# The first block's input stage done chunk by chunk, its loads moved to other queues, and a rewritten sliding softmax

## The reference

```
h = rms_norm(x, norm1_g) * (1 + scale1) + shift1
proj = h @ w_in                       # q_g k_g v_g a_lr r_g q_s k_s v_s
log_a = log_sigmoid(a_lr @ w_alpha + b_alpha) / 16
o_gla = rms_norm(gla_mixer(q_g, k_g, v_g, log_a)) * silu(r_g)
o_swa = rms_norm(swa_mixer(q_s, k_s, v_s, sinks))
x = x + gate1 * (concat(o_gla, o_swa) @ w_out)
x = x + gate2 * peer_mixer(modulate(x, ...))     # 256 x 8 x 16 expert rows looked up in a table
```

## Time and profile before

| | us |
|---|---|
| median of 3 runs | 1480.1 (1479.36 to 1480.94) |
| profiled execution: its own time, which is its span | 1480.7 |
| PE busy | 1311.9 (89%) |
| DVE busy | 933.9 (63%) |
| ACT busy | 655.4 (44%) |
| stage that the change touches | 0 to about 122 us of the span |

### The profile page before, as it was taken

How to read it: one execution, slowest core, us unless ns; L and a number is a source line. 1 busy time by engine, 2 the same in 40 slices (tenths; PEclk the granted TensorE clock), 3 DMA queues, 4 the chain that set the end, 5 groups by cost and what they waited for, 6 DMA issues and landing times.

```text
span 1480.7 us, 21207 instructions
## 1 busy us (share of the span) xinstructions
PE 1311.9 (89%) x6932; PEld 936.0 (63%) x6932; DVE 933.9 (63%) x2248; ACT 655.4 (44%) x1801; POOL 390.6 (26%) x432
## 2 busy tenths in 40 slices
PE   6999979888988777878777887999999998999998
PEld 3889934444443222333222476999998987899897
DVE  6678586766667667667754555655556635655555
ACT  3434434344343333333333335545455248544554
POOL 4111144444544444444444142200001005100000
PEclk9999999999999999999999998999999999999999
DMA  8875599999999999999999621665556630445554
GB/s 332 333 254 200 182 422 420 421 421 421 421 421 422 421 422 421 422 421 422 421 422 421 268 89 37 234 219 182 182 182 238 196 102 14 157 149 188 187 185 144
DMA packets 81341, 422.51 MB, mean 285 GB/s; under 512 B 10144, under 2 KB 11472, under 8 KB 48368
## 3 DMA queue, kind: packets, MB, share of 16 engines
q0 software_dynamic: 46656, 303.71, 50.1%
q1 hardware_dynamic: 33280, 114.68, 23.3%
q10 hardware_dynamic: 1328, 3.15, 0.6%
HBM read 418.88 MB, written 2.62 MB: 285 GB/s over the span
## 4 chain that ended last, share of the span: by engine, by line
PE 55%; DMA 27%; DVE 8%; ACT 5%; issue 2%; POOL 1%; DVEq 0%; ACTq 0%; SPq 0%; POOLq 0%
DMA big<-in_experts,R 26%; PE pacc L1136 8%; PE pu L663 6%; PE pu L664 6%; PE pu L665 6%; PE pu L632 3%; DVE big L2380 3%; PE pu L644 2%; PE pacc L663 2%; PE pacc L664 2%; PE pacc L665 2%; PE pacc L720 2%; PE pacc L722 2%; PE pacc L721 2%; ACT L1455 1%
## 5 line engine op out<-in xcount | busy, mean ns | idle before, releaser
L1136 PE MATMUL pacc<-big,early_l 128*128 128x512 f32 x1024 | 492.7, 622 | 119.5 <-ACT early_l L1455 119.2
L1136 PEld LDWEIGHTS pacc<-big,early_l 128*128 128x128 f32 x1024 | 188.1, 195 | 408.4 <-issue 406.1
L2380 DVE CUSTOM_DVE_ANT_0 big<-big,early_h 128x1024 f32<-128x1024 f32 x256 | 311.8, 1224 | 204.9 <-DMA big<-in_experts,R 203.8
L535 POOL DMA_INDIRECT big<-in_experts,R x256 | 288.1, 1125 | 378.7 <-PE pacc L1136 334.3
L436 DVE TENSOR_TENSOR ring_lo<-ring,ring_hi 128x512 fp32r<-128x512 f32 x328 | 214.7, 696 | 195.0 <-ACT ring_hi L429 194.9
L429 ACT ACTIVATE ring_hi<-ring 128x512 fp32r<-128x512 f32 x328 | 187.6, 620 | 123.5 <-PE pu L665 49.4
L1455 ACT ACTIVATE R<-R 128x1 f32<-128x1 f32 x256 | 51.6, 202 | 322.3 <-DVE R L2380 322.1
L663 PE MATMUL pu<-X2h,ring_hi 128*128 128x256 f32 x512 | 146.2, 286 | 3.2 <-DVE big L2497 3.2
L665 PE MATMUL pu<-X2h,ring_lo 128*128 128x256 f32 x512 | 145.6, 284 | 0.0
L664 PE MATMUL pu<-X2l,ring_hi 128*128 128x256 f32 x512 | 145.4, 284 | 0.0
L663 PEld LDWEIGHTS pu<-X2h,ring_hi 128*128 128x128 f32 x512 | 98.9, 193 | 4.2 <-DVE big L2497 3.6
(11 more groups left out here) (408 smaller groups left out, 2097.4 us busy)
## 6 DMA issues: line engine op xcount, KB each, us to landing
ring<-in_weights SPq DMA_DIRECT2D x216, 512.0 KB, 3.5
big<-in_ada POOLq DMA_DIRECT2D x40, 512.0 KB, 6.3
big<-in_w POOLq DMA_DIRECT2D x12, 512.0 KB, 7.1
big<-in_experts,R POOLq DMA_INDIRECT x256, 20.0
bias_row<-big ACTq DMA_DIRECT2D x1, 1536.0 KB, 19.8
XT<-in_xT ACTq DMA_DIRECT2D x1, 1024.0 KB, 8.2
scr<-in_ada POOLq DMA_DIRECT2D x2, 512.0 KB, 12.3
tk<-in_ada POOLq DMA_DIRECT2D x2, 512.0 KB, 14.0
```

The lines of the kernel that those rows point to most:

```text
L535: pool.indirect_dma_start(out=pair_rows[:, m % PAIR_SLOTS, :], out_offset=None, in_=experts_d, in_offset=bass.IndirectOffsetOnAxis(ap=expe ...
L1136: last = mm(paccf[:, tt * D + half * 512:tt * D + (half + 1) * 512], diagonal[:, m % 16, :], pair_rows[:, m % PAIR_SLOTS, D + half * 512:D ...
L2380: v.tensor_tensor_reduce(out=pair_rows[:, m % PAIR_SLOTS, 0:D], in0=pair_rows[:, m % PAIR_SLOTS, 0:D], in1=h2_rows[:, u % TT, :], scale=1. ...
```

## The change

1. Eight chunks of `w_in` (q, k, v of the sliding mixer and q of the linear one) are laid out by chunk of x: slot c has the rows of chunk c for 8 output tiles. PE adds all 8 tiles in PSUM (`pacc`) as each chunk comes, the narrow product with them. ACT copies 8 tiles out at the end. `EARLY` becomes 8, `BESIDE` 9.
2. The 16 first modulation rows come as 8 pairs of 1 MB, loaded from ACT's queue, with columns, bias table and one-hot table in front; c, x in two halves and weight slots 0 to 7 from SP's queue; the other small loads from POOL's.
3. The bias row is made by one product for 8 partitions, and the store repeats each row 128 times by a step of 0.
4. 24 matmuls on zeros stand at PE's start. The sum of squares is taken in two halves. DVE scales x chunk by chunk.
5. Sliding softmax: ACT makes a table of slope times distance per head; DVE makes the negated logits with their minimum in one instruction (`negative_logits`) and a one-column minimum with the negated sink.
6. The decay arithmetic of DVE becomes filler of steps 0 to 5, in front of it nothing; the exponentials of ACT come in three parts after slots 10 to 12. Modulation rows fill steps 6 to 16, five follow.

```diff
-EARLY, BESIDE = 6, 11
+EARLY, BESIDE = 8, 9
+EXPS_AFTER = 10
@@ SP
-            for dst, src, sem in ((cols[:, :], cols_d, "cols_loaded"), ...
-            for k in range(RING):
-                if k < 2:
-                    sp.wait_ge(s["ada_used"], 8 + 4 * k)
-                sp.dma_start(ring[:, k, :], weights_d[k, :, :]).then_inc(slot_full[k], 16)
+            sp.dma_start(cs, c_d.partition_broadcast(P)).then_inc(s["c_loaded"], 16)
+            for half, sem in enumerate(("x_loaded", "x_late_loaded")):
+                sp.dma_start(XT[:, 4 * half:4 * half + 4, :], xT_d[:, 4 * half:4 * half + 4, :]).then_inc(s[sem], 16)
+            for c in range(C):
+                if c >= RING:
+                    sp.wait_ge(s["slots_used"], c + 1 - RING)
+                ring_load(c)
@@ POOL
-            for n_row in range(2 * C):
-                pool.dma_start(mod_row(n_row), ada_d[n_row, :, :]).then_inc(ada_first[first_part(n_row)[0]], 16)
+            for dst, src in ((walr, small_d[:, :, 0:16]), (walpha[0:16, :], alpha_d), (sinks[:, :], sinks_d.partition_broadcast(P)),
+                             (keysT, keys_d)):
+                pool.dma_start(dst, src).then_inc(s["small_loaded"], 16)
@@ PE
+            full_array(24, pu[:, 1, 0:T])
+            pe.wait_ge(s["cols_loaded"], 16 * 3)
+            mm(pu[0:NH, 0, 0:BROW], relb[0:NB, 0:NH], oneh[0:NB, :], start=True, stop=True).then_inc(s["row_psum"], 1)
...
+            pe.wait_ge(s["small_loaded"], 16 * 4)
+            pe.wait_ge(s["row_copied"], 1)
             for c in range(C):
                 pe.wait_ge(s["h_chunks"], c + 1)
+                last = mm(pn[0:16, 0:T], walr[:, c, :], HTf[:, c, :], start=(c == 0), stop=(c == C - 1))
...
+                wait_slot(c)
+                w = slot(c)
+                for j in range(7):
+                    last = mm(pacc[:, j, :], w[:, j * P:(j + 1) * P], HTf[:, c, :], start=(c == 0 and j % 2 == 0),
+                              stop=(c == C - 1), skip_group_check=True)
+                    if c == C - 1 and j == 4:
+                        log_decay()
+                for tt in range(TT):
+                    last = mm(pacc[:, 7, tt * P:(tt + 1) * P], HTf[:, c, tt * P:(tt + 1) * P], w[:, 7 * P:C * P], start=False,
+                              stop=(c == C - 1), skip_group_check=True)
+                last.then_inc(s["slots_used"], 1)
@@ ACT
+            for dst, src in ((cols[:, :], cols_d), (relb[0:NB, :], relb_d), (oneh[0:NB, :], onehot_d)):
+                act.dma_start(dst, src).then_inc(s["cols_loaded"], 16)
+            for c in range(6):
+                pair_load(c)
...
+            act.wait_ge(s["row_psum"], 1)
+            f(brow[0:NH, 0, :], pu[0:NH, 0, 0:BROW], ACT.Copy).then_inc(s["row_copied"], 1)
             act.wait_ge(s["sums"], NORM["n1"])
             f(R[:, 0:TT], pn[:, 0:TT], ACT.Sqrt, scale=1.0 / D, bias=eps[:, 0:1]).then_inc(s["roots"], 1)
+            act.wait_ge(s["row_copied"], 1)
+            row = brow[0:NH, 0, 0:1]
+            act.dma_start(row_dram, bass.AP(tensor=row.tensor, offset=row.offset, ap=[list(row.ap[0]), [0, P], [1, BROW]]))\
+                .then_inc(s["row_stored"], 16)
+            for c in range(6, C):
+                act.wait_ge(ada_pair[c - 6], 16)
+                pair_load(c)
+            act.wait_ge(s["consts_made"], 1)
+            for h in range(SH):
+                f(swa_table[:, h, :], ndist, ACT.Copy, scale=2.0 ** (-8.0 * (h + 1) / SH))
             for c in range(C):
                 act.wait_ge(s["h_scaled"], c + 1)
                 f(HTf[:, c, :], HTf[:, c, :], ACT.Identity, bias=mod[:, 2 * c + 1:2 * c + 2], ...
...
+            act.wait_ge(s["slots_used"], SLOT["w_in"] + C)
+            for j in range(4):
+                f(qs[:, j, :], pacc[:, j, :], ACT.Copy, scale=float(SD) ** -0.5).then_inc(s["evacs"], 1)
+            f(ks, pacc[:, 4, :], ACT.Copy).then_inc(s["evacs"], 1)
...
@@ DVE
+            def normed_chunk(c):
+                dve.wait_ge(s["ada_used"], 2 * c + 2)
+                v.tensor_tensor(mod[:, 2 * c:2 * c + 2], mod[:, 2 * c:2 * c + 2], first[:, 2 * c:2 * c + 2], ALU.add)
+                v.scalar_tensor_tensor(HTf[:, c, :], XT[:, c, :], column("n1", c), pm[:, 0:T], ALU.mult, ALU.mult)\
+                    .then_inc(s["h_scaled"], 1)
+            modulation(0, 2)
+            dve.wait_ge(s["roots"], NORM["n1"])
+            v.reciprocal(R[:, 0:TT], R[:, 0:TT]).then_inc(s["inverses"], 1)
+            modulation(2, 2)
+            dve.wait_ge(s["spreads"], 1)
+            normed_chunk(0)
+            normed_chunk(1)
+            for c in range(2, C):
+                modulation(2 * c, 2)
+                normed_chunk(c)
...
+            def negative_logits(u, S, ps, added):
+                v.tensor_tensor_reduce(out=S, in0=ps, in1=added, scale=-1.0, scalar=3.0e38, op0=ALU.add, op1=ALU.min,
+                                       accum_out=stats[:, u % 4:u % 4 + 1]).then_inc(s["att_biased"], 1)
...
-                v.tensor_copy(Ssw[:, u % 4, L:L + 1], sinks[:, h:h + 1])
-                v.scalar_tensor_tensor(S, ndist[:, T - L:T], 2.0 ** (-8.0 * (h + 1) / SH), ps, ALU.mult, ALU.add)\
-                    .then_inc(s["att_biased"], 1)
+                negative_logits(u, S, ps, swa_table[:, h, T - L:T])
             def swa_filler(i):
-                if i < 12:
-                    modulation(2 * C + 6 + i, 1)
-                if 8 <= i < 8 + 3 + NSUB:
-                    gla_product(i - 8)
+                if i < 6:
+                    decay_part(i)
+                else:
+                    modulation(2 * C + i, 1)
+                if 11 <= i:
+                    gla_product(i - 11)
+                if i == 16:
+                    gla_product(i - 10)
...
-            modulation(2 * C + 18, 4)
+            modulation(2 * C + 17, 5)
```

More of the change, by code:

```diff
@@ L97 @@
 NORM = {n: i + 1 for i, n in enumerate(NORMS)}
[L98 removed]
+SQUARED = {n: i + 2 for i, n in enumerate(n for n in NORMS if n not in ("n2", "n2_late", "fin", "attn0", "lat", "mlp0", "attn1", "mlp1"))}
 def attention_units():
@@ L797, in attend, with full_array @@
                     one(step)
+            def full_array(count, out):
+                for _k in range(count):
+                    mm(out, zeros[:, 0:P], zeros[:, :], start=True, stop=True)
             pe.wait_ge(s["casts_made"], 1)
[L801 to L804, removed]
+            full_array(24, pu[:, 1, 0:T])
+            pe.wait_ge(s["cols_loaded"], 16 * 3)
+            mm(pu[0:NH, 0, 0:BROW], relb[0:NB, 0:NH], oneh[0:NB, :], start=True, stop=True).then_inc(s["row_psum"], 1)
+            for c in range(C):
+                if c % 4 == 0:
+                    pe.wait_ge(s["squares"], SQUARED["n1"] - 1 + c // 4)
+                for tt in range(TT):
+                    last = mm(pn[:, tt:tt + 1], sq[:, c, tt * P:(tt + 1) * P], ones[:, 0:1], start=(c == 0 and tt == 0),
+                              stop=(c == C - 1), skip_group_check=True)
             last.then_inc(s["sums"], 1)
@@ L916, in _ @@
             swa_step(swa_steps)
-            def full_array(count, out):
-                for _k in range(count):
-                    mm(out, zeros[:, 0:P], zeros[:, :], start=True, stop=True)
             def swa_sums():
@@ L2036, in _ @@
-            for c in range(3, C):
+            normed_chunk(0)
+            normed_chunk(1)
+            for c in range(2, C):
                 modulation(2 * c, 2)
-                dve.wait_ge(s["ada_used"], 2 * c + 2)
-                v.tensor_tensor(mod[:, 2 * c:2 * c + 2], mod[:, 2 * c:2 * c + 2], first[:, 2 * c:2 * c + 2], ALU.add)\
-                    .then_inc(s["h_scaled"], 1)
-            dve.wait_ge(s["h_chunks"], C)
+                normed_chunk(c)
+            dve.wait_ge(s["h_scaled"], C)
@@ L2042, in _ @@
             v.memset(stats[:, 0:1], 0.0).then_inc(s["normed"], 1)
+            dve.wait_ge(s["small_loaded"], 16 * 4)
+            for half in range(2):
+                v.tensor_scalar(strided(Ssw[:, half, P:P + 1], [[2 * 264, 4], [P, 2]]), strided(sinks[:, 4 * half:4 * half + 1], [[1, 4], [0, 2]]),
+                                -1.0, None, ALU.mult)
             modulation(2 * C, 6)
-            dve.wait_ge(s["la_parts"], 1)
-            step(v.scalar_tensor_tensor(la, zb, 0.0, zln, ALU.min, ALU.subtract))
```

236 lines of the change are left out of this document (104 added, 132 removed).

## The result

The change made the kernel slower: 1505.8 us in the median of four runs (1504.4 to 1507.0) against 1479.9, ratio 1.0178, 95% interval 1.0163 to 1.0192. The profiled execution spans 1504.8 us, 24.1 more than that of before. The forecast was 1476.0, with a range to 1484.

What follows compares the result with a forecast made beforehand. PE's gapless chain and DVE both bound the first reciprocal, near 121 us. Summing start, chunk loop and DVE's steps gave 117.5 for 121.6, a gain of 4.1: 1480.7 to 1476.6, less 0.6 for the median, 1476.0; range 1467 to 1484.

Steps and rivals of the forecast that it cites:

- Bounds for the two are 0.8 and 4.2, I take 2.0: On ACT ahead of chunk 0: issuing pairs 6 and 7 behind the row store takes 2.0 us together.
- Bounds for the store are 4.1 alone and 19.8: Row store in ACT's queue ahead of pairs 6 and 7: taken nearest to its packets' sum, 4.1 us.
- the rule on engines: Row store: an outermost dimension of 8 confines it to at most 8 engines, so 8.2 us in place of 4.1.
- The rival of late pairs: Slow store in ACT's queue delays pairs 6 and 7: loop ends 6.8 us later, time 1483; chance 0.22, blocked ACT included.
- The sum otherwise: Whole start: chunk 0 at 22.5, loop end at 57.2, `la_parts` at 64.7, `gla_ops` at 105.7, DVE ready at 117.5 us.
- the forecast's 117.5: First reciprocal after the first block's mixers: DVE ready at 117.5 us against 121.6 before, a gain of 4.1.
- The forecast's step of 0.6: End of the sum: profiled run lies 0.6 us above the median, so 1476.6 becomes 1476.0.
- the rival on PE: Up to the first reciprocal: DVE's waits melt away, PE bounds at 108.2, a gain of 11.1, time 1469; chance 0.25.
- The thread behind the loop: DVE from `la_parts` at 64.7 through decay pieces and attention steps: 41.0 us, to `gla_ops` at 105.7.
- DVE becomes the thread: Behind the chunk loop: decay arithmetic moves inside steps 0 to 5, so DVE's work sets the time to the reciprocal, 117.5.
- the two engines reach 121 us together: Kernel before, first reciprocal: PE's chain ends at 121.59, DVE is free at 121.07, so faster PE alone gains nothing.
- eight bias rows (10.55 us of PE) go: Start on PE, ahead of the narrow product: 10.55 us of bias rows vanish; one product hides in the wait for x.

Runs made afterwards that it cites:

- e_step12: The changed kernel with 12 copies of each bias row, the store reading eight partitions that lie 12 apart; ratio 1.0094 to the kernel before.
- e_pairs_first: The changed kernel, its slow store kept, with pairs 6 and 7 issued ahead of the store in ACT's queue; ratio 1.0077 to the kernel before.
- e_both: The changed kernel with pairs 6 and 7 issued ahead of the store and the store reading 128 partitions; ratio 1.0025 to the kernel before.
- e_fill_both: e_fill_norm with 20 more products of zeros on PE in front of the scores of units 10 and 11; ratio 0.9980 to the kernel before.
- e_fill_norm: e_both with 12 products of zeros ahead of chunk 0 and 26 in place of 6 between the two norms; ratio 0.9998 to the kernel before.

## Why the prediction was wrong

**The step that failed** is the one on ACT behind the root: "Bounds for the two are 0.8 and 4.2, I take 2.0" for the issues of pairs 6 and 7. They took 21.6 us. I had priced an issue as a fixed piece of work, from the `keys` load; the runs show a wait that follows what stands ahead in the queue (9.0 us behind a fast store, 21.6 behind the slow one, about 1 with no store ahead), and the store could not move before six pairs were through. With it failed "Bounds for the store are 4.1 alone and 19.8", where I took the sum of its packets at the price of the earlier trace rows. That price is one of packets from 128 partitions. The store took 30 us, beyond both bounds, and the rule on engines that I weighed beside it gave 8.2: it speaks of the number of engines only, and 12 apart it would have been right (8.4 in e_step12).

**The rival of late pairs** had place and sign, and 0.22. It named a stall of ACT in its issues as one of its two ways, and this way was the whole: pairs 6 and 7 landed at 62 and 66 (forecast 40.0 and 43.9), but PE, at chunk 0 only at 43.3, did not wait for them. Its price of 6.8 us was too small by 20, for the same two terms.

**The sum otherwise** closes to the span, to 0.1 us by luck, as the last part varies by 5 between traces. Chunk 0 came 20.8 late: 19.6 by the issues, 0.9 each by the root and the store's own issue, 0.6 back elsewhere. From chunk 0 to slot 8 the loop took 38.2 for 34.7: the low clock 2.6 for 2.0, 4.20 a chunk for 4.09, the product for `log_a`, 1.1, which the sum had left out, the ring 0.7. From there to the first reciprocal it took 62.8 for 60.3. Together 26.8 over the forecast's 117.5, and with 1.5 between the norms 28.3: 1476.6 + 28.3 is 1504.9. The forecast's step of 0.6 from the profiled run to the median compares a span with a time; the gain of 4.1 does not hang on it. In the rival on PE, 108.2 leaves out the sums and the root (2.2), which its gain of 11.1 holds.

**Right** were x at 12.4, chunk 0 at 22.5 once the issues are free (22.55 in e_pairs_first; 22.33 in e_both, there with some luck: the root came 1.1 later than in the sum and the three issues took 1.0 less), Ln's end 7 us behind the loop (7.5 forecast), the steps 0 to 5, the later stages. The sum of squares ended at 17.05, at the far bound of 17.0: its first half took 2.76 us and its second 3.57, which is half of the 6.97 of before; the granted clock was 0.79 from 10 to 12 us and 0.50 from 12 to 18, so what the 24 products of zeros had raised was gone again for the second half. **The thread behind the loop**: from Ln's end to the last decay product DVE took 41.0 in the sum and 43.3 after (44.3 in e_both). In e_both the first six steps took 12.0 for 12.2; the excess stands in the steps behind them. At least 1.5 us of it was the low clock: e_fill_both, with zeros in the hole ahead of slot 13, took 41.7 where e_fill_norm took 43.2, so the step costs of the sum were nearly right. "DVE becomes the thread" was half right: it waits for ACT and ACT for PE, in a ring.

**What I overlooked in the earlier trace rows**: that the two engines reach 121 us together also means that PE has no hole there. I took a PE that is ahead of DVE for harmless. And "eight bias rows (10.55 us of PE) go" counted as gain what lay in a wait for DVE's rows. So the forecast of 1476 would have failed without the store as well, by 7 us (e_both). That e_fill_both comes to 1476.7 does not bear it out: it needs products of zeros that the change does not have.

## What to carry to other kernels

Before a transfer from few partitions goes ahead of something urgent in a queue, ask two things: behind which ports these partitions lie, and whether the issuing engine has work behind its next issue, since that issue may wait until the transfers ahead have moved. Put the urgent loads first and the bulk last. When an edit makes PE earlier at a place where another engine is the later one, look at the granted clock behind the new wait: here, behind holes of 2.3 to 3.1 us, the work up to the next step took 1.5 to 3 us more, and products of zeros in the holes gave it back.

## What the hardware showed that I had not expected

- An issue on ACT's queue took up to 17.2 us (pair 6) where the usual one takes 0.3 to 1.3, behind a store of 1024 pieces that waited itself. In four kernels ACT was free 9.0 to 21.6 us after, the later the slower the store; with the fastest store both issues were over before its first packet moved. That fits an issue that waits for room in the queue; what holds it was not tried apart.
- The same 1536-byte packet takes 65, 118 or 225 ns by the distance of the eight source partitions (12, 16 or 1 apart).
- Taking 9 us of work off PE made the kernel 2 us slower at the first reciprocal, and 50 small products of zeros put the same time back.
